# Two prompt groups of 1024 instead of three unequal ones in a gate-and-up stage, with the samples' products taken out of them

## What is computed

```python
x = x + jnp.concatenate([o_att, o_ml], axis=-1) @ w_out
h2 = rms_norm(x, norm_ffn_w)
g, u = jnp.split(h2 @ w_ffn_in, 2, axis=-1)          # 1024 -> 2 * 2816
gp = jnp.concatenate([conv_buf.astype(g.dtype), g], axis=1)
gc = conv_b + gp[:, 0:T] * conv_w[0] + gp[:, 1:T + 1] * conv_w[1] + gp[:, 2:T + 2] * conv_w[2]
x = x + (jax.nn.silu(gc) * u) @ w_down               # 2816 -> 1024
new_conv = gp[:, -(CONV_W - 1):]
```

## Time and profile before

| | us |
|---|---|
| median of 3 runs | 2361.06 |
| lowest and highest | 2359.53 and 2365.66 |
| the profiled execution | 2364.47 |
| its span | 2362.7 |
| gate-and-up stage in it, first to last matmul | 887.1 to 1929.1 |
| down stage in it | 1931.4 to 2358.0 |
| PE busy / DVE busy / POOL busy / ACT busy | 2253.2 / 1620.8 / 1034.6 / 899.3 |
| mean granted TensorE clock | 0.985 |

### The profile page before, as it was taken

How to read it: one execution, slowest core, us unless ns; L and a number is a source line. 1 busy time by engine, 2 the same in 40 slices (tenths; PEclk the granted TensorE clock), 3 DMA queues, 4 the chain that set the end, 5 groups by cost and what they waited for, 6 DMA issues and landing times.

```text
span 2362.7 us, 34413 instructions
## 1 busy us (share of the span) xinstructions
PE 2253.2 (95%) x13423; PEld 1984.9 (84%) x13423; DVE 1620.8 (69%) x2271; ACT 899.3 (38%) x1524; POOL 1034.6 (44%) x811
## 2 busy tenths in 40 slices
PE   7999999999999998888879999989999999999999
PEld 6899878887777888777768999988999998888887
DVE  5666655556573457888878899888998974445653
ACT  4555622222232324444444444444444433233331
POOL 4333312222121346655554666655666630245730
PEclk9999999999999998999998999999999999999999
DMA  8433222222154553444344333353333345686454
GB/s 283 151 126 121 79 86 81 81 81 67 45 183 142 192 184 122 156 139 138 132 161 140 117 118 116 118 181 100 119 118 119 119 158 190 219 289 202 139 177 165
DMA packets 208076, 333.95 MB, mean 141 GB/s; under 512 B 23083, under 2 KB 148679, under 8 KB 205847
## 3 DMA queue, kind: packets, MB, share of 16 engines
q1 hardware_dynamic: 207883, 331.69, 41.5%
q0 software_dynamic: 32, 0.07, 0.0%
HBM read 235.42 MB, written 97.24 MB: 141 GB/s over the span
## 4 chain that ended last, share of the span: by engine, by line
PE 65%; DVE 7%; DMA 5%; issue 4%; POOL 3%; ACT 3%; SPq 0%; DVEq 0%; POOLq 0%; ACTq 0%
PE bank L114 12%; PE bank L115 12%; PE bank L116 12%; PE bank L2803 9%; PE bank L2804 8%; PE bank L2805 8%; DMA late_c_raw<-in_w_ffn_in_dram 3%; DVE late_t L3184 1%; DVE late_s_act L3154 1%; DVE late_t_lo L3129 1%; POOL late_c_raw L3381 1%; POOL late_t_raw L3385 1%; DVE late_t L3187 1%; DMA late_a_raw<-h_parts 1%; ACT late_t_hi L2930 1%
## 5 line engine op out<-in xcount | busy, mean ns | idle before, releaser
L2803 PE MATMUL bank<-late_a_hi,late_b_hi 128*128 128x384 f32 (+1 forms) x1056 | 350.0, 331 | 56.3 <-issue 18.6
L2804 PE MATMUL bank<-late_a_lo,late_b_hi 128*128 128x384 f32 (+1 forms) x1056 | 344.7, 326 | 0.0
L2805 PE MATMUL bank<-late_a_hi,late_b_lo 128*128 128x384 f32 (+1 forms) x1056 | 343.2, 325 | 0.0
L2803 PE MATMUL bank<-late_a_hi,late_t_hi 128*128 128x384 f32 (+1 forms) x792 | 262.9, 332 | 19.6 <-DVE late_gp L3172 8.5
L2803 PEld LDWEIGHTS bank<-late_a_hi,late_b_hi 128*128 128x128 f32 x1056 | 201.7, 191 | 69.1 <-issue 36.3
L2804 PE MATMUL bank<-late_a_lo,late_t_hi 128*128 128x384 f32 (+1 forms) x792 | 258.3, 326 | 0.0
L2805 PE MATMUL bank<-late_a_hi,late_t_lo 128*128 128x384 f32 (+1 forms) x792 | 257.6, 325 | 0.0
L114 PE MATMUL bank<-late_e_hi,late_y_a_hi 128*128 128x512 f32 x616 | 242.1, 393 | 2.1 <-DVE late_e_lo L3202 2.1
L116 PE MATMUL bank<-late_e_hi,late_y_a_lo 128*128 128x512 f32 x616 | 242.6, 394 | 0.0
L115 PE MATMUL bank<-late_e_lo,late_y_a_hi 128*128 128x512 f32 x616 | 241.7, 392 | 0.0
L3379 POOL TENSOR_TENSOR late_t_raw<-late_c_raw 128x512 f32<-128x512 f32 x64 | 84.2, 1315 | 327.9 <-DMA late_c_raw<-in_w_ffn_in_dram 300.4
(11 more groups left out here) (380 smaller groups left out, 5187.1 us busy)
## 6 DMA issues: line engine op xcount, KB each, us to landing
late_c_raw<-in_w_ffn_in_dram SPq DMA_DIRECT2D x64, 1024.0 KB, 5.1
late_y_a_raw<-act_parts SPq DMA_DIRECT2D x77, 512.0 KB, 3.6
late_e_raw<-in_w_down_dram SPq DMA_DIRECT2D x77, 256.0 KB, 4.1
act_parts<-late_s_act SPq DMA_DIRECT2D x22, 768.0 KB, 4.4
att_next_hh<-h_parts SPq DMA_DIRECT2D x16, 1024.0 KB, 4.8
late_d_raw<-in_w_down_dram SPq DMA_DIRECT2D x11, 1024.0 KB, 7.6
late_a_raw<-h_parts SPq DMA_DIRECT2D x14, 768.0 KB, 12.7
act_parts<-late_t SPq DMA_DIRECT2D x22, 384.0 KB, 2.5
```

The costliest lines, as they stand in the source:

```text
L2803: nc.tensor.matmul(out, w_h, hi[:, c, :], start=first, stop=False, skip_group_check=True)
L2804: nc.tensor.matmul(out, w_h, lo[:, c, :], start=False, stop=False, skip_group_check=True)
L2805: ins_ = nc.tensor.matmul(out, w_l, hi[:, c, :], start=False, stop=last, skip_group_check=True)
```

## The change

- The stage has two groups, each of 1024 prompt tokens: 22 steps instead of 33, 512 moving columns in every matmul of a unit.
- The samples leave the groups. In the first group's 11 steps `sample_unit(r, u)` follows each unit: the plain product with the same split weights, 4 block products of 4 chunks by 3 matmuls, 48 matmuls with 64 moving columns. `keep_z`, `add_s`, `conv_head_s`, `tap_s` (DVE, 4 a step), `silu_of_s` and `gate_s` do for the 64 columns what the group's instructions did; `store_as` writes the result.
- The samples' down product, now `down_s(n)` with 6 matmuls, stands inside each unit of the second group behind product 4 (n of 4). Its operands are loaded (`load_ds`, `load_as`), rounded and split (`split_ds`, `split_as`) in that group's steps.
- Weights are loaded in place: `c_raw` is gone, `load_b` writes `b_raw`, which is also `b_lo`. The load for unit u of a step waits until unit u of the step before (and its `sample_unit`) is through. All four `split_b` of a unit wait for all four sums.
- `t` has one buffer, and `s_act` lies in the buffer of `up`: `conv_head` and `keep_first` of the up unit wait until the step before has been stored (`w_act_out`).
- Both engines' lists in a step are written in another order. POOL: `gate` ahead of the sums for unit 1. DVE: the four `sum_act` ahead of the splits of unit 1.
- The first group's activations: four positions more are kept in `a_raw`, their sums (`first_a`) are made at positions 10 to 13 instead of 6 and 7, and they are rounded and split at the last position and in the first step, because `a_hi` lies where the output projection's weights are. Before, this was done at positions 7 to 14.

```diff
-ORDER = (0, 1, 2, 3, NT, 4, 7, 5, 8, 6, 9, 10, 13, 11, 14, 12, 15)
+FIRST_AT = 8
+ORDER = (0, 1, 2, 3, NT, 4, 5, 6, 7, 8, 12, 9, 13, 10, 14, 11, 15)
-GROUPS = [Group(0, 0, SAMPLE_AT * P, NS, (0, 2)), Group(1, 512, 768, 0, (2, 5)), Group(2, 1280, 768, 0, (5, 8))]
+GROUPS = [Group(0, 0, SEQ // 2, (0, 4)), Group(1, SEQ // 2, SEQ // 2, (4, 8))]
...
         def load_b(u, r):
-            if turn(r) >= 1:
-                w_split(sp, before(r), 4 * u + 3)
+            p = before(r)
+            w_prod(sp, p, 7 * u + 6)
+            if has_s(p):
+                w_prod_s(sp, p, u)
...
         def unit(r, u):
                 ins_.then_inc(prod, 1)
+                if G.index == 1 and n == 4:
+                    down_s(2 * i + u)
+        def sample_unit(r, u):
+            w_sadd(pe, r if u else before(r), 1 - u)
+            for q, (b, half) in enumerate(((B11, 0), (B21, 1), (T1, 0), (B22, 1))):
+                out = s_cols(u, min(q, 2))
+                for c in range(KH):
+                    w_h, w_l = b_parts(u, b, c)
+                    n = slice((half * KH + c) * NS, (half * KH + c + 1) * NS)
+                    nc.tensor.matmul(out, w_h, hs_hi[:, n], start=q < 3 and c == 0, stop=False, skip_group_check=True)
+                    nc.tensor.matmul(out, w_h, hs_lo[:, n], start=False, stop=False, skip_group_check=True)
+                    ins_ = nc.tensor.matmul(out, w_l, hs_hi[:, n], start=False, stop=q != 2 and c == KH - 1, skip_group_check=True)
...
 # DVE, one step
+            if has_s(p):
+                add_s(p, 1)
-            if p is not None:
-                split_b(r, 1, 0)
             combine(r, 0, 0)
-            if p is not None:
-                split_b(r, 1, 1)
+            sum_act(p, 0)
+            sum_act(p, 1)
             combine(r, 0, 1)
-            split_b(r, 1, 2)
+            sum_act(p, 2)
+            sum_act(p, 3)
+            if G.index == 1:
+                split_ds(2 * i)
+                split_as(i)
+            split_b(r, 1, 0)
             combine(r, 0, 2)
...
 # POOL, one step
-            sums_b(r, 1)
             if p is not None:
                 gate(p, 0)
                 gate(p, 1)
-                heads(r)
-            tails(r)
-            sums_b(after(r), 0)
+            if has_s(p):
+                gate_s(p)
+            heads(r)
+            sums_b(r, 1)
+            tails(r)
+            sums_b(after(r), 0)
```

More of the change, by code:

```diff
@@ L2313, in late @@
     y_x = put("y_x", at_a, [P, 2, 2, HJ, 512])
-    y_u = put("y_u", at_a + 64 * D, [P, HJ, 512])
+    y_u = put("y_u", at_y_u, [P, HJ, 512])
+    FIRST, LAST = (groups[0], 0), (groups[-1], NP - 1)
+    positions = [Position(n) for n in range(LAST_AT + 1)]
+    final = positions[-1]
     rows_in, rows_laid, cols_laid = (k.sem(n) for n in ("rows_in", "rows_laid", "cols_laid"))
@@ L2375, in after @@
         return (groups[n // NP], n % NP) if n < len(groups) * NP else None
-    FIRST, LAST = (groups[0], 0), (groups[-1], NP - 1)
-    positions = [Position(n) for n in range(LAST_AT + 1)]
-    final = positions[-1]
     s_dram = h2_dram[:, 1].rearrange("p c n -> p (c n)")
     def h_of(p):
-        return h_t[(p.c - SAMPLE_AT - 1) % 2 + 2 * (p.c > LAST_AT - 2)]
+        return h_t[(p.c - FIRST_AT - 1) % 2 + 2 * (p.c > LAST_AT - 2)]
     def s_of(p):
@@ L2473, in kept_parts @@
     def kept_parts(p, b):
-        if p.c > SAMPLE_AT:
+        if p.sample:
+            return [(hs_raw[:, b * KH * NS:(b + 1) * KH * NS].rearrange("p (c r) -> p c r", r=NS), 0, NS)]
+        if p.c > FIRST_AT:
             return [(h_of(p)[:, b * 512:(b + 1) * 512].rearrange("p (c r) -> p c r", r=P), 0, P)]
[L2477 to L2484, removed]
+        G = groups[0]
+        slot, col = ((A11, A12), (S3, A22))[p.tile // 4][b], p.tile % 4 * P
+        return [(A_raw(slot, G)[:, :, col:col + P], 0, P)]
     def w_turned(eng, n):
@@ L2815, in sample_down, with down_s @@
+        def down_s(n):
+            i, x = n // 2, n % 2
+            if n == 0:
+                w_sadd(pe, (groups[0], NP - 1), 1)
+                pe.wait_ge(rows_kept, 2)
+            if x == 0:
+                pe.wait_ge(acts_split, i + 2)
+            pe.wait_ge(d_split, n + 1)
             for g in range(2):
-                for x in range(2):
-                    cs = slice(x * D + g * 512, x * D + (g + 1) * 512)
-                    ins_ = mm3(nc, bank[6 + g][0:NS, :], acts_hi[:, x, :], acts_lo[:, x, :], d_hi[:, cs], d_lo[:, cs],
-                               i == 0 and x == 0, i == NP - 1 and x == 1)
+                cs = slice(g * 512, (g + 1) * 512)
+                ins_ = mm3(nc, bank[6 + g][0:NS, :], acts_hi[:, x, :], acts_lo[:, x, :], d_hi[:, cs], d_lo[:, cs],
+                           n == 0, n == 2 * NP - 1)
@@ L2873, in _ @@
                 unit(r, 0)
-                if G.index == 1 and i == 0:
+                if has_s(r):
+                    sample_unit(r, 0)
+                unit(r, 1)
+                if has_s(r) and i == NP - 1:
                     turn_conv_s()
-                    pe.wait_ge(rows_kept, 2)
-                unit(r, 1)
-                p = before(r)
-                if p is not None and p[0].sample:
-                    sample_down(p)
+                if has_s(r):
+                    sample_unit(r, 1)
         turn_conv_p()
@@ L3110, in norm_x @@
             x_var.mark(nc.vector.tensor_scalar(xvar[0:r, :], xss[0:r, :], 1.0 / D, EPS, ALU.mult, ALU.add))
+        def norm_x(p):
+            r = p.rows
             x_rstd.wait(dve, p)
@@ L3272, in step @@
                 split_a(nxt[0], 0)
-            combine(r, 1, 3)
+            combine(r, 1, 2)
             if nxt is None:
@@ L3305, in _ @@
             if p is final:
-                for q in range(3):
+                for q in range(4):
                     split_b(FIRST, 0, q)
+                split_a(groups[0], 0)
             add_x(p, 1)
-            if p is final:
-                split_b(FIRST, 0, 3)
             if p.c == 0:
                 ml_end.divide(dve, ml_end.last)
-            norm_x(p)
+            if p is final:
+                split_a(groups[0], 1)
+            var_x(p)
+            if p is final:
+                split_a(groups[0], 2)
+            else:
+                norm_x(p)
             if p.c == 0:
@@ L3349, in first_a @@
             out, x, y, op = A_SUMS[n]
-            h_kept.wait(pool, positions[SAMPLE_AT])
+            h_kept.wait(pool, positions[FIRST_AT])
             wait(pool, a_summed, n)
```

599 lines of the change are left out of this document (330 added, 269 removed).

## The result

The changed kernel takes **2414.68 us** (median of 4 runs, 2410.91 to 2422.08), the kernel before 2362.86 beside it: ratio 1.0224, 95% interval 1.0195 to 1.0253. It is slower by 52 us, and outside the range forecast. The profiled execution has a span of 2412.6, which is 49.9 above the one before.

What follows compares the result with a forecast made beforehand. PE was taken to bound the steady second group, a circle of waits the first. PE work 994.5 + waits 21 + 13 + start 10 + turn 6 = 1044.5 against 1042.1 us, so 2363 us, range 2339 to 2390.

Steps and rivals of the forecast that it cites:

- Together 848 + 30.5 + 116 = 994.5 us: PE's work in the changed gate-and-up stage: unit matmuls, `down_s` and sample matmuls, against a present stage of 1042.1 us.
- the three rivals: Whole kernel: faster by sample overlap or lower pace and waits (0.37); slower by late weights (0.14); slower by longer waits.
- the second and third: Slower rivals, 0.36 together: weights too late, 2396 or 2429 us; all counted waits somewhat longer, about 2390 us.
- my signs of being wrong: New profile: sample spacing below 0.09 or above 0.13, `late_gp` waits at product 6 every gate unit, or no step waits.
- Unit matmuls: Both groups' units: 3696 matmuls of 512 columns at 0.2295 us, 848 us (839 to 853).
- Samples' spacing: First group's `sample_unit`: 1056 matmuls of 64 columns, 0.110 us apart, set by weight loads, 116 us (43 to 120).
- The rival of 0.041: Samples' matmuls overlap better, 0.041 us each, 73 us less, kernel at 2290 us; chance 0.06.
- Second-group waits: PE waits 1.3 us a step before `down_s` and 0.6 in unit 1; 1.9 x 11 = 21 us.
- First-group waits: Unit 1: `tap_s` delays `combine` 1 to 39.8, PE wants it at 38.6; 1.2 x 11 = 13 us.
- The start and the turn: Stage start: roundings and splits cost 10 us; group turn: delayed `combine` 2 and first `down_s` cost 6 us.
- Outside the stage: Nothing moved on the path: projection positions stay with PE despite longer POOL sums; down stage keeps its 1848 matmuls.
- Rival 2 (weights late): Both groups' steps: in-place loads delay POOL's sums, a split and the third `combine`; 2396 or 2429 us; chance 0.14.

Runs made afterwards that it cites:

- experiment 2: Changed kernel with each sample matmul streaming its 64 columns twice, into 128 PSUM columns, the copy unused: 2374.7 us, ratio 1.0048 to the kernel before.
- experiment 4: Changed kernel with `split_ds` and `split_as` ahead of the third and fourth `sum_act` in DVE's second-group list: 2403.46 us, ratio 1.0189 to the kernel before.
- experiment 5: Changed kernel with POOL's `pair_s` ahead of `first_a` in the positions before the stage: 2413.46 us, ratio 1.0222 to the kernel before.

## Why the prediction was wrong, step by step

**The step that failed is the price of PE's work**, "Together 848 + 30.5 + 116 = 994.5 us": matmuls at the pace of 0.2295 and samples at 0.110, all at full clock. I had read 1.00 in the steady windows and carried it over to a stream that the kernel before doesn't have, although its own groups as a whole were granted 0.97 to 0.99. A clock term was put at nothing: 48 us by the count of slow matmuls, of which 42.5 come from the sample runs (experiment 2). With the clock of experiment 2 (0.99) the changed kernel's stage is 1047.3 us long. I had forecast 1044.5. None of the three rivals named this either: the second and third have the sign, the second by a wait that did not come, the third by longer waits, and the waits were shorter than forecast. None of my signs of being wrong named the clock; they looked at spacing and waits.

With that clock the terms came out as follows.

- **Unit matmuls.** Forecast 848; 0.2317 each in the second group by experiment 4 and 0.2324 in the first by experiment 2, together 858 (+10). My value lay between the two rows; the truth is at or just above the higher one.
- **Samples' spacing.** Forecast 0.110 and 116 us. They come 0.112 apart, the first two of a run 0.03 to 0.05, so that a run takes 5.3 us up to the next unit and the 22 runs 117 (+1). The argument from the rate of weight loads held: 64 and 128 moving columns come at the same spacing. The rival of 0.041 is out, and so is the 86 us by the Trainium skill (TensorE: Matmul & The Clock Gate, Back-to-back issue gap), whose 81 ns per matmul no run of sample matmuls here reaches.
- **Second-group waits.** Forecast 1.9 a step; 0.8 (experiment 4), all ahead of `down_s` as said. Steps took 42.5, forecast 43.2. Over eleven steps that is 9 us instead of 21 (-12).
- **First-group waits.** Forecast 13 us; none in the steady steps (-13). The four `tap_s` took 2.94 us together in a row of DVE's timeline of the changed kernel, and the `combine` into `up` behind them ended 14.1 us after the unit's start, not 15.0, just as PE got there:

```profile
1211.51 2.94 DVE L3253 SCALAR_TENSOR_TENSOR late_t_s<-late_gs,late_cc,late_t_s 128x64 f32<-128x64 f32 x4
1214.38 0.68 DVE L3284 TENSOR_TENSOR late_up<-bank,late_up 128x512 f32<-128x512 f32 x1
```

 Steps at full clock took 49.7 (experiment 2); forecast 50.3. With the clock as it was they took 51 to 60.
- **The start and the turn.** Forecast 10 and 6. In experiment 2 PE's first unit starts 4.4 us after the projection ("issue") and the first step is 15.8 us above a steady one: 20. The two steps around the turn are 13 us above theirs. Both ends are twice what I put (+10 and +7); the 27 slow matmuls of experiment 2 lie in them.
- **Outside the stage.** "The projection's positions ... stay with PE" was wrong by 3.3 us: I named POOL's longer sums and did not follow SP's queue behind them. The down stage kept its time, as said.
- **Rival 2 (weights late).** It did not come. In the steady steps of the first group PE is busy without a break, and in those of the second it waits for `late_acts_lo` alone.

So the small terms err by +10, +1, -12, -13, +10 and +7. That they nearly cancel (+3) is luck, and the omitted clock term of over 40 us decides. With it in, the forecast for the same working would have been about 2363 + 42.5 = 2405 and more.

The Trainium skill (TensorE: Matmul & The Clock Gate, HAM oscillation) has the clock fall over idle gaps of PE, as when it waits for a DMA. By that section nothing would fall here. This case's trace disagrees: 0.91 in 162.80 us in which PE was busy 162.80, and 1.00 once the same matmuls streamed 128 columns. How the chip comes to its level within a run is not shown. It was not the same for every run: in the changed kernel several runs pass at full speed and the large matmuls behind them are slow, and the pattern differs between the traces of experiment 5 and of the changed kernel, whose gate-and-up stages have the same matmuls.

## What to carry to other kernels

Before moving work into small matmuls, price not only their spacing but the clock that the kernel gets with them: PE can be busy 100% and do part of its work at half its speed. Read the granted clock in windows of a few steps, above all for a stretch where PE is busy throughout and two equal pieces of work differ in length. If small matmuls can't be avoided, give them more columns where that is free (here two operands that lie side by side, 32 matmuls for 48), keep runs short, and put large matmuls between them.

## What the runs showed of the hardware

- A gapless stream of fp32r matmuls of 64 columns with new 128-column weights each comes 0.11 us apart, and with 128 columns too: here the second 64 columns were free.
- With runs of 48 such matmuls between the units the granted clock was 0.96 and 0.91 over three steps each, with PE idle for 0.1 us in all, and 0.86 over two steps with a wait of 2.4 us; 128 columns, 12 matmuls a run in place of 48, or the same 48 spread in groups between large ones kept it at 1.00 from 1000 to 1200 us, where the changed kernel had 0.96.
- At 1.2 GHz the small matmuls come 0.21 us apart and those of 512 columns 0.43, both about double: the spacing of the small ones, which columns do not set, grows with the lower clock too.
- A `norm_x` of 128 x 1024 on DVE took 2.3 us in one position and 5.6 in another beside POOL's `first_a` of 4.6. That the two hold each other up was not tried by itself.
